# Attention units of a two-block transformer kernel: transposes split around the scores, output parts taken from PSUM by ScalarE and VectorE

## The reference

```python
def diff_attend(q, k, v, lam, g_subln, lam_init):
    s = jnp.einsum('bqhcd,bkhcd->bchqk', q.astype(jnp.float32), k.astype(jnp.float32)) * ATTN_SCALE
    p = jax.nn.softmax(s, axis=-1)
    w = p[:, 0] - lam * p[:, 1]
    o = jnp.einsum('bhqk,bkhd->bqhd', w, v.astype(jnp.float32))
    o = o * lax.rsqrt(jnp.mean(o * o, axis=-1, keepdims=True) + EPS) * g_subln.astype(jnp.float32)
    return (o * (1.0 - lam_init)).astype(v.dtype)
```

## Time and profile before

| | |
|---|---|
| median of 3 runs | 3063.06 us (3061.89 to 3063.12) |
| the profiled execution | 3062.65 us |
| its span | 3061.0 us |
| PE busy | 2918.3 us, 95% of the span |
| weight loads of PE busy | 2362.6 us, 77% |
| VectorE busy | 1772.6 us, 58% |
| ScalarE busy | 1435.6 us, 47% |
| GpSimd busy | 526.8 us, 17% |
| mean granted clock of TensorE | 0.986 |

### The profile page before, as it was taken

One profiled execution on the slowest core, in us unless ns is written; L12 is line 12 of the kernel. 1 busy time (PEld: TensorE's weight loads), 2 busy tenths in 40 slices (PEclk: granted clock), 3 DMA queues, 4 the chain that ended last, 5 costly groups with the idle time before them and its releaser, 6 DMA issues. The chain is left out here.

```text
span 3061.0 us, 38462 instructions
## 1 busy us (share of the span) xinstructions
PE 2918.3 (95%) x15438; PEld 2362.6 (77%) x15438; DVE 1772.6 (58%) x1996; ACT 1435.6 (47%) x1913; POOL 526.8 (17%) x626
## 2 busy tenths in 40 slices
PE   8999999998999899999999899999999998899998
PEld 4878887786887578777777378788888896688887
DVE  4438846445545788888888364555544316455543
ACT  3345627346223478888787133533333325433332
POOL 0006514123101632222222100000000002000000
PEclk9999999999999999999999999999999999999999
DMA  5221011023753589999999551233332301233331
GB/s 208 56 64 42 15 36 56 28 56 97 220 179 110 202 326 372 363 365 373 375 386 354 225 194 42 56 98 97 104 103 69 114 24 47 76 98 95 91 103 42
DMA packets 278385, 456.07 MB, mean 149 GB/s; under 512 B 24864, under 2 KB 206752, under 8 KB 258112
## 3 DMA queue, kind: packets, MB, share of 16 engines
q1 hardware_dynamic: 251712, 398.82, 37.8%
q0 software_dynamic: 26496, 54.79, 4.9%
HBM read 451.16 MB, written 39.08 MB: 160 GB/s over the span
## 5 line engine op out<-in xcount | busy, mean ns | idle before, releaser
L266 DVE TENSOR_TENSOR weight_part<-weights,weight_part 128x2048 fp32r<-128x2048 f32 (+1 forms) x61 | 138.3, 2267 | 157.4 <-ACT weight_part L255 157.4
L1188 ACT ACTIVATE up_conv<-banks,tap_columns 128x512 f32<-128x512 f32 x88 | 68.5, 778 | 292.4 <-PE banks L313 292.4
L255 ACT ACTIVATE weight_part<-weights 128x2048 fp32r<-128x2048 f32 (+1 forms) x61 | 114.1, 1870 | 169.6 <-PE banks L308 164.1
L776 POOL TENSOR_SCALAR branch_mean<-branch_mean 128x1 f32<-128x1 f32 x20 | 10.4, 521 | 1057.2 <-ACT up_conv L770 713.3
L1232 DVE SCALAR_TENSOR_TENSOR up_conv<-banks,tap_columns,up_conv 128x511 f32<-128x511 f32 x88 | 66.0, 750 | 218.0 <-ACT up_conv L1188 218.0
L308 PE MATMUL banks<-hT_r,weight_part 128*128 128x512 f32 x432 | 171.1, 396 | 1.8 <-DVE weight_part L266 1.4
L313 PE MATMUL banks<-hT_r,weight_part 128*128 128x512 f32 x432 | 169.9, 393 | 0.0
L266 DVE TENSOR_TENSOR weight_part_o<-weights,weight_part_o 128x2048 fp32r<-128x2048 f32 (+2 forms) x46 | 100.0, 2175 | 117.8 <-ACT weight_part_o L255 117.8
L308 PE MATMUL banks<-hT_r,weight_part_o 128*128 128x512 f32 x384 | 151.0, 393 | 0.0
L313 PE MATMUL banks<-hT_r,weight_part_o 128*128 128x512 f32 x384 | 150.2, 391 | 0.0
L312 PE MATMUL banks<-h_low,weight_part_o 128*128 128x512 f32 x384 | 149.1, 388 | 0.0
(11 more groups left out here) (742 smaller groups left out, 8874.9 us busy)
## 6 DMA issues: line engine op xcount, KB each, us to landing
weights<-in_w_e_gate SPq DMA_DIRECT2D x44, 1024.0 KB, 15.3
weights<-in_w_e_up SPq DMA_DIRECT2D x44, 1024.0 KB, 13.6
hT<-in_w_e_down SPq DMA_DIRECT2D x44, 1024.0 KB, 11.9
weights<-in_w_up SPq DMA_DIRECT2D x88, 512.0 KB, 5.1
gate_up<-in_w_e_gate SPq DMA_DIRECT2D x22, 1024.0 KB
gate_up<-in_w_e_up SPq DMA_DIRECT2D x22, 1024.0 KB
down<-in_w_e_down SPq DMA_DIRECT2D x22, 1024.0 KB
weights<-in_w_down SPq DMA_DIRECT2D x20, 1024.0 KB, 5.0
```

The source lines that it names most:

```text
L255: c.nc.scalar.activation(self.pair(n)[0][:, 0:z], self.raw[n % RAW_SLOTS][:, 0:z], ACT.Copy).then_inc(self.high_ready, 1)
L266: c.nc.vector.tensor_tensor(low[:, 0:z], self.raw[n % RAW_SLOTS][:, 0:z], high[:, 0:z].bitcast(F32), ALU.subtract).then_inc(self.low_ready, 1)
L1188: nc.scalar.activation(a[:, f % 2, v], c.ps[:, 2 * (f % 4) + v], ACT.Identity, scale=conv[:, 2, ch:ch + 1], bias=bias[:, ch:ch + 1]).then_ ...
```

## The change

It does three things in `diff_units`.

1. On PE, transposes 0 to 3 of unit j stand first in a step, ahead of the first half of the scores, and wait for `mixed` alone. Transposes 4 and 5 stay behind that half; they wait for `boxed`, and now for `out_low` in place of `out_full`. The product with v waits for both copies before its first tile and takes tiles 0 to 5 in order.
2. On ScalarE, the copy of tiles 0 to 3 stands ahead of that of tiles 4 and 5.
3. The full output is no longer stored. ScalarE writes the high part straight from PSUM times the gain, and VectorE writes the low part straight from PSUM, as gain times value minus high part, between the ratio and the mix. GpSimd's subtraction and its wait for `out_low` in `parts` are gone.

```diff
@@ GpSimd
-            def low(j):
-                pool.wait_ge(out_high, j + 1)
-                nc.gpsimd.tensor_tensor(place(o_low_r, j), place(o_low, j), place(o_high, j).bitcast(F32), ALU.subtract).then_inc(out_low, 1)
-
             def parts(i):
...
-                if i >= 9:
-                    pool.wait_ge(out_low, i - 8)
...
-            for i in range(U + 8):
+            for i in range(U + 5):
...
-                if i >= 8:
-                    low(i - 8)
@@ PE
             for i in range(U + 6):
                 j = i - 3
+                if 0 <= j < U:
+                    pe.wait_ge(mixed, j + 1)
+                    for b in range(4):
+                        last = nc.tensor.transpose(c.ps[:, 6, b * P:(b + 1) * P], pr[:, j % 3, 0, b * P:(b + 1) * P], c.ident[:])
+                    last.then_inc(turned, 1)
                 if i < U:
...
                     scores_of(i, 0)
                 if 0 <= j < U:
-                    pe.wait_ge(mixed, j + 1)
                     if j:
                         pe.wait_ge(boxed, j)
                     if j >= 4:
-                        pe.wait_ge(out_full, j - 3)
-                    for b in (4, 5, 0, 1, 2, 3):
-                        last = nc.tensor.transpose(c.ps[:, 6 + b // 4, (b % 4) * P:(b % 4 + 1) * P], pr[:, j % 3, 0, b * P:(b + 1) * P], c.ident[:])
-                        if b == 5:
-                            last.then_inc(turned_end, 1)
-                    last.then_inc(turned, 1)
+                        pe.wait_ge(out_low, j - 3)
+                    for b in (4, 5):
+                        last = nc.tensor.transpose(c.ps[:, 7, (b - 4) * P:(b - 3) * P], pr[:, j % 3, 0, b * P:(b + 1) * P], c.ident[:])
+                    last.then_inc(turned_end, 1)
...
                 if j >= U:
                     pe.wait_ge(boxed, U)
-                    pe.wait_ge(out_full, j - 3)
+                    pe.wait_ge(out_low, j - 3)
                     turn_out(j - 3)
                 elif j >= 0:
                     h = units[j][1]
                     pe.wait_ge(copied_end, j + 1)
                     if j >= 3:
                         turn_out(j - 3)
-                    for b in (4, 5, 0, 1, 2, 3):
-                        if b == 0:
-                            pe.wait_ge(copied, j + 1)
-                        last = nc.tensor.matmul(c.ps[:, 7, 2 * P:3 * P], prT[:, j % 2, b], v[:, b, h * P:(h + 1) * P], start=b == 4, stop=b == 3)
+                    pe.wait_ge(copied, j + 1)
+                    for b in range(6):
+                        last = nc.tensor.matmul(c.ps[:, 7, 2 * P:3 * P], prT[:, j % 2, b], v[:, b, h * P:(h + 1) * P], start=b == 0, stop=b == 5)
                     last.then_inc(summed, 1)
@@ ScalarE
-            def take_out(m):
+            def high_out(m):
                 act.wait_ge(out_turned, m + 1)
-                nc.scalar.activation(place(o_low, m), c.ps[:, 7, 3 * P:4 * P], ACT.Copy, scale=gcol[:]).then_inc(out_full, 1)
-
-            def high_out(m):
-                act.wait_ge(out_full, m + 1)
-                nc.scalar.activation(place(o_high, m), place(o_low, m), ACT.Copy).then_inc(out_high, 1)
+                nc.scalar.activation(place(o_high, m), c.ps[:, 7, 3 * P:4 * P], ACT.Copy, scale=gcol[:]).then_inc(out_high, 1)
...
                 if 0 <= j < U:
-                    act.wait_ge(turned_end, j + 1)
+                    act.wait_ge(turned, j + 1)
                     if j >= 2:
                         act.wait_ge(summed, j - 1)
+                    nc.scalar.activation(prT[:, j % 2, 0:4].rearrange("p t n -> p (t n)"), c.ps[:, 6], ACT.Copy).then_inc(copied, 1)
+                    act.wait_ge(turned_end, j + 1)
                     nc.scalar.activation(prT[:, j % 2, 4:6].rearrange("p t n -> p (t n)"), c.ps[:, 7, 0:2 * P], ACT.Copy).then_inc(copied_end, 1)
-                    act.wait_ge(turned, j + 1)
-                    nc.scalar.activation(prT[:, j % 2, 0:4].rearrange("p t n -> p (t n)"), c.ps[:, 6], ACT.Copy).then_inc(copied, 1)
                 if e < U:
                     act.wait_ge(maxed, e + 1)
                     if e >= 3:
-                        act.wait_ge(turned, e - 2)
+                        act.wait_ge(turned_end, e - 2)
...
                 if j >= 3:
-                    take_out(j - 3)
+                    high_out(j - 3)
@@ VectorE
+            def low_out(m):
+                dve.wait_ge(out_high, m + 1)
+                nc.vector.scalar_tensor_tensor(place(o_low_r, m), c.ps[:, 7, 3 * P:4 * P], gcol[:], place(o_high, m).bitcast(F32), ALU.mult, ALU.subtract).then_inc(out_low, 1)
+
-            for i in range(1, U + 5):
+            for i in range(1, U + 7):
...
                     L(nc.vector.scalar_tensor_tensor(ratio[:, k % 2:k % 2 + 1], rl[:, k % 4, 1:2], lam[:], ls[:, k % 3, 0:1], ALU.mult, ALU.mult))
+                    if i >= 7:
+                        low_out(i - 7)
                     nc.vector.scalar_tensor_tensor(pr[:, k % 3, 0], pr[:, k % 3, 1], ratio[:, k % 2:k % 2 + 1], pr[:, k % 3, 0], ALU.mult, ALU.add).then_inc(mixed, 1)
+                elif i >= 7:
+                    low_out(i - 7)
```

More of the change, by code:

```diff
@@ L2686, in diff_units @@
         lifted, rooted, scaled = c.sem("du_lifted"), c.sem("du_rooted"), c.sem("du_scaled")
-        out_turned, out_full, out_high = c.sem("du_out_turned"), c.sem("du_out_full"), c.sem("du_out_high")
+        out_turned, out_high = c.sem("du_out_turned"), c.sem("du_out_high")
         out_low = c.sem("du_out_low")
@@ L2841, in _ @@
                     nc.scalar.activation(sq, ob[:, j % 3], ACT.Square, scale=P ** -0.5, accum_out=ss[:, j:j + 1]).then_inc(squared, 1)
-                if j >= 3:
-                    high_out(j - 3)
                 if i == U - 4:
@@ L2849, in _ @@
             L = lambda ins: c.vlink(dve, ins)
-            for i in range(1, U + 5):
+            def low_out(m):
+                dve.wait_ge(out_high, m + 1)
+                nc.vector.scalar_tensor_tensor(place(o_low_r, m), c.ps[:, 7, 3 * P:4 * P], gcol[:], place(o_high, m).bitcast(F32), ALU.mult, ALU.subtract).then_inc(out_low, 1)
+            for i in range(1, U + 7):
                 e, k, m = i - 1, i - 2, i - 5
-                if m >= 0:
+                if 0 <= m < U:
                     dve.wait_ge(rooted, m + 1)
```

## The result

| | before | after |
|---|---|---|
| median | 3063.06 us (7 runs, 3060.37 to 3068.37) | 3071.15 us (7 runs, 3067.37 to 3077.03) |
| ratio after to before, 95% interval | | 1.003 (1.0017 to 1.0043) |
| profiled execution, its span | 3062.65, 3061.0 | 3067.37, 3065.7 |
| mean granted clock, profiled execution | 0.986 | 0.986 |

The changed kernel is slower by 8 us, where +1 was forecast and 3069.0 was the upper end.

What follows compares the result with a forecast made beforehand. Attention steps of 4.20 us were bound by PE and one ring of waits through ScalarE. Terms -1.0 - 0.55 + 1.2 + 0.9 = +0.55 a block, +1.1 us for both, gave 3064.0 us; range 3060 to 3069.

Steps and rivals of the forecast that it cites:

- The exponentials' ring: Waits from exponentials through scores, transposes and copies back to exponentials: 4.20 us a step before, forecast 3.65, no longer binding.
- first three steps: Start of each block, with no output part yet: 3.87 instead of 4.20 us a step, -1.0 us a block.
- eight middle steps: Middle of each block: steps between 4.04 and 4.40 us, taken as 4.13 instead of 4.20, -0.55 us a block.
- step of L266: Step where VectorE also makes a weight part: 5.41 us where PE before went on after 4.22, +1.2 us a block.
- closing steps: Three closing steps of a block: later wait (+0.4) and fewer transposes behind it (-0.44 us) even out.
- last outputs: End of each block, outputs going one by one through VectorE's subtraction: +0.9 us a block.
- The clock term: Half-clock stretch on PE after the block: if it begins or ends otherwise, 1.5 us either way.
- PE alone binds: Rival: VectorE never comes last, steps are 4.04 us, total -1 or -3, 3060 to 3062 us; chance 0.20.
- Lock step: Rival: VectorE's mix holds GpSimd's add every step, steps of 4.40 to 4.48 us, total +7.7, 3070 us; chance 0.16.
- Full gain: Rival: PE's gaps close fully and the ends are free, -6.4 us, 3056 us; chance 0.04.
- the second ring: Waits from output product through ScalarE's copy and VectorE's subtraction to two transposes and back: 4.00 us if VectorE is in time.

Runs made afterwards that it cites:

- e6: Changed kernel plus eleven filling matmuls on PE in the gap before the third unit's scores of each block; median 3064.24 us, ratio 0.9997 to before.
- e5: Kernel before plus eleven filling matmuls on PE in the gap before the third unit's scores of each block; median 3065.60 us, ratio 1.0003.
- e4: Kernel before plus two casts on GpSimd at the end of each block, delaying what follows; median 3067.02 us, ratio 1.0002.
- e1: Changed kernel measured again, no edit; median 3071.64 us, ratio 1.0014 to before.
- e2: Changed kernel with output parts made as before, leaving only the new order of transposes and copies; median 3062.16 us, ratio 0.9987 to before.
- e9: Changed kernel once more, unaltered, in the third series; median 3071.41 us, ratio 1.0015 to before.
- e3: Changed kernel with PE and ScalarE in the old order, leaving only the new output parts; median 3082.04 us, ratio 1.0053 to before.
- e10: Repeat of e6, the changed kernel with filled starts, in the third series; median 3065.36 us, ratio 0.9995 to before.
- e11: Repeat of e5, the kernel before with filled starts, in the third series; median 3067.05 us, ratio 0.9997 to before.
- e7: As e2, only the new order of transposes and copies, plus filled block starts; median 3052.54 us, ratio 0.9962 to before.
- e8: As e7, plus filling matmuls (4, 3, 3 and 6) among each block's last output transposes; median 3056.72 us, ratio 0.997 to before.
- e12: As e10, but GpSimd does not add epsilon to the mean square; median 3069.07 us, ratio 1.0 to before.

## Why the prediction was wrong

**What bounds the steps**: right. The exponentials' ring is gone, two transposes wait for the subtraction, the subtraction takes 0.35 as estimated from the rows. The estimate from the Trainium skill (VectorE: DVE Perf Modes, section on the TRN2 errata), 62 cycles more for a PSUM source, was 0.41; the measurement decides against it. The reasoning behind the 0.35 was weaker than it looked: a line through one row with SBUF sources and one with a PSUM source can't show that both have the same fixed part, it assumes it. Only the new row shows it: 0.35 for 128 and 0.75 for 511 columns, both from PSUM, give 1.04 ns a column and 0.22 fixed, and the mix from SBUF (1.02 for 768) lies on the same line.

**The terms of the sum.** Measured best with filled starts, first block, e6 against e5, since nothing of the clock lies in it:

| term | forecast | measured |
|---|---|---|
| first output a little earlier | (not in the sum) | -0.22 |
| first three steps | -1.0 | -0.89 |
| eight middle steps | -0.55 | -0.35 |
| step of L266 | +1.2 | +1.02 |
| closing steps | 0 | +0.29 |
| last outputs | +0.9 | +0.74 |
| block | +0.55 | +0.61 |

The sum is right, and in part by luck: errors of 0.1 to 0.3 cancel. The mixture of 4.05 and 4.35 was foreseen as "between 4.04 and 4.40"; I took 4.13 "because a long round ends by itself", but it also begins again by itself, every second step, so a pair of steps has the mean 4.20. The term is -0.35 and not nothing because in the eight steps more short ones than long ones came. In the closing steps the later wait and the fewer transposes do not even out fully.

**The clock term: this is the step that failed.** I wrote "it is 1.5 us either way", and looked for it behind the block. Three things are wrong there. (1) It is not the same for both orders. With the usual start, 3.4 us at half clock, the block is longer by 0.9 (87.91 against e4's first block without its casts, 87.06) and by 1.4 (87.96 against 86.59), together **+2.2** instead of the 1.3 with filled starts (and the 1.1 forecast). (2) It has a tail to one side: of eight unfilled starts of blocks with the new PE order that were profiled (after, e1, e2, e9), two had 10.2 us at half clock, which cost 2.5 (e2) and 2.8 us (e1); of six with the old order (before, e3, e4) none had, and one had 7. That is too few for a rate, and too few to say that the order of PE makes the tail. (3) It was looked for in one place, while the clock moves the whole program: executions of one and the same kernel differ by up to 21 us (before in the third series, 3057.00 to 3077.57), with the mean clock.

**The size.** The three series of the unaltered changed kernel (means +8.5 +- 1.7, +6.0 +- 1.8, +3.7 +- 1.2 against before) make +5.5 +- 0.9 when weighted by their errors; 2.2 of it are in the steps with their starts. Two long starts in eight would add 1.3, and the old order's one start of 7 us in six takes back 0.4. The remaining 2 us or so are not located. So chance has its part in the miss too: the first series is the highest of the three, and +5.5 on its 3063.06 would have been 3068.6, just inside the range. In the first pair of profiles 2.7 us came from a half-clock stretch at 1898 us, far behind the change:

```profile
1892.00:1902.00 10.00, 9.07 (x40) 5.60 (x39) 4.65 (x13) 5.07 (x8) 0.00 (x0) 0.82 0.78 265
1902.00:1912.00 10.00, 10.00 (x58) 7.95 (x58) 4.54 (x12) 3.68 (x6) 0.00 (x0) 0.84 0.14 50
```

e1 and e6 had it too, which looked like a mark of the change, until e9 and e10 did not have it and e11, the kernel before with its filling, did (0.88 and 0.78). It comes and goes from execution to execution, so it is no mark of the change.

**The rivals.** "PE alone binds" is out (transposes wait in every second step); its sum also had -0.9 for eight steps of 0.16 less, which make -1.3, but nothing hangs on that. "Lock step" is out for the changed kernel: the hold is real (1.01 for the add beside the mix, 0.22 ahead of it), but it comes every second step only. Its time, 3070, came close to the result for another reason. "Full gain" is out, and e2 shows what took it: mainly the output parts' place on VectorE (83.07 us a block without it, 87.91 with it), of which the ends are only 0.74. Without the second ring PE's steps stand free at 3.97, where I had bounded them by 4.04 from below.

**Still open**: by what way the start costs the new order more. That the difference goes away when the start is filled is shown by e1 and e2 against e6 and e7, by e9 against e10, and by e5 and e11, where the old order gains nothing. The rows of the blocks account for 2.5 of the 5.0 us between e9 and e10; whether the rest is the rarer long stretch, or a different clock in the program behind, no run here shows. Nor is it shown that the order of PE makes the low clock at a start last longer. It wasn't tried to change only the place of the four transposes in the first units.

## What to carry to other kernels

When a change moves waits of PE by tenths of a microsecond, the steps can be costed to 0.1 us a block and the median still be missed, because the granted clock behind PE's gaps can be worth more than the steps (here +2.2 with the usual starts against +1.3 with filled ones, and more in the means); look for gaps of some microseconds at the start and in the middle of a stage, and try filling them, before judging an order. Judge orders with such gaps filled and the mean clock beside each time. And an operation moved onto an engine that has time on average still costs where its round is the longest: here a subtraction of 0.35 on VectorE, and PE's wait for it, took back what a better order on PE had won.

## What the runs showed of the hardware

- Filling a gap of 2.7 us with matmuls that nobody needs kept the granted clock at 1.00 in all fourteen block starts profiled with it, where without it each of fourteen had 3.4 us or more at 0.50. It shortened the executions only with the new order of PE (5.0 +- 1.7, e10 against e9), not with the old (0.5 +- 1.0, e5 and e11 against before).
- A one-column operation on GpSimd that starts 0.22 ahead of VectorE's mix takes 0.22; one that starts 0.08 behind it takes 1.01, to just past the mix's end. Two engines fall into a pattern of period two by this (4.05, 4.35), which ended when the add was taken out (e12, 4.05).
- A higher mean clock is not in itself a shorter time: e8 raised the mean clock from 0.9870 to 0.9884 and its time did not fall below e7's.
- Faster steps can go with a fall of the clock inside the block that costs more than they saved (e12, 0.83 in 524 to 534 us: blocks of 86.96 and 87.46 against 86.65 and 86.69). In e12 and e3 it followed each of four waits of PE of 1.54 to 1.56 us, in the others one of sixteen of 1.37 to 1.40.
- The fixed part of a VectorE operation is the same 0.22 us with a PSUM source (0.35 for 128 columns, 0.75 for 511) as with SBUF sources (1.02 for 768).
